# The sample tokens' depthwise convolution as one product over all shifts, one sum and one bias per chunk

## The chip, the cores and the metric

The kernel runs on one core of one Trainium2 chip. The metric is the device time of one execution in microseconds (us): the median of three runs of the kernel before is 1164.72 us (1164.26 to 1165.55). Input layout on the host is not timed.

## What is computed

One inference step of one decoder layer, for 512 prompt tokens (one sequence) and 64 sample tokens (8 sequences of 8 steps), all in float32, model width 1024:

```
x   = x + 0.5 * gate1 * SwiGLU_1(mod(rmsnorm(x)))
hm  = rmsnorm(x) * (1 + scale) + shift
proj = hm @ w_in                       # a, g (512 channels each) and u_pool (512)
u_conv   = a * sigmoid(g)
conv_ext = concat(conv_prev, u_conv)   # 30 earlier positions: zeros for the prompt, a state for the samples
v   = depthwise_causal_conv(conv_ext, w_dw) + b_dw      # 31 taps, every channel by itself
v   = silu(layernorm(v))               # over the 512 channels
p   = multi-scale pooling of u_pool
x   = x + gate * (concat(v, p) @ w_out)
x   = x + 0.5 * gate2 * SwiGLU_2(mod(rmsnorm(x)))
y   = rmsnorm(x)
```

Outputs are y for prompt and samples, and the last 30 (15) inputs of the convolution (pooling) as new states. The change concerns the line of the depthwise convolution, and of it the part of the 64 sample tokens.

## The kernel before, in words

Channels lie on the 128 partitions, tokens along the free dimension. A chunk is 128 channels; the 512 channels of the convolution are chunks 0 to 3. The 576 tokens lie in two halves of 288, each with 256 prompt columns and 32 sample columns; `prompt(t)` and `sample(t)` are views of these. The program is written by hand for each engine, in the order in which the engine runs it, with semaphores between the engines. The matrix products are float32 made of three passes (high by high, low by high, high by low), with weights split on ACT (`split_hi`, L599) and GpSimd (`split_lo`, L1118) and brought by SP's DMA queue in units of 128x2048.

The stage that matters here is the mixer, between the first and the second feed-forward part. TensorE computes six units of w_in; units 0, 2, 4 and 5 of these (`GLU`) hold a and g of chunks 0 to 3, units 1 and 3 the pooling's input. VectorE (DVE) runs this list, in this order (L1058 to L1079):

- `glu(c)` (L1024, L1026) multiplies sigmoid and TensorE's result into `conv_p` (prompt, 30 + 512 columns for each chunk) and `conv_s` (samples, 30 + 8 steps of 8 sequences = 304 columns for each chunk, step by step, the 8 sequences side by side). It frees the PSUM tile for TensorE's next unit (`tile_read[1]`).
- `conv_start(c)` (L1041, L1042) is tap 0 with the bias, one instruction for the 512 prompt columns and one for the 64 sample columns.
- `conv_taps(c, g0, g1)` (L1052, L1055) is the taps 1 to 30, in groups of 5, as a loop of DVE (`dve.Fori`) with the window's address and the wait's value computed in registers. Each tap is a scalar_tensor_tensor, v = window * w + v, for the prompt (L1052) and one for the samples (L1055). Each signals `conv_tap`, and each waits for the one before it of its own kind, since it adds to what that one wrote. A loop of a single group is written out without registers.
- The list is: glu 0, chunk 0 with glu 1 before its last group, chunk 1 with glu 2 before its last two groups, glu 3, chunk 2, an evacuation of modulation values, and of chunk 3 tap 0 and one group. The other 25 taps of chunk 3 are made by TensorE (`conv_batch`, L511, L513) as products with diagonal matrices that ACT makes (`diagonals`, L772), again one product for the prompt's 512 columns and one for the 64 sample columns. L1078 and L1079 add them.
- TensorE's `ln_sum(c)` (L525) sums a chunk over its channels as soon as it is complete. After the last one come DVE's centring (L1085), ACT's squares (L822), TensorE's sums over the tokens (L398), and the scaling, and then the product with w_out (`out_chunk`), whose chunks 0 to 3 are from the pooling and 4 to 7 from v.

GpSimd meanwhile splits weights (L1118) and makes the pooling's window sums and means (L1189 to L1229). Nothing in the program orders GpSimd's instructions against DVE's taps.

## Time and profile before

| | |
|---|---|
| median of 3 runs | 1164.72 us (1164.26 to 1165.55) |
| profiled execution: its span, first to last instruction | 1163.8 us |
| its own time beside the span | not given apart; the runs lie 0.5 to 1.8 us above the span, the median 0.9 us |
| TensorE busy | 1102.1 us, 95% |
| VectorE busy | 380.0 us, 33% |
| ScalarE busy | 317.3 us, 27% |
| GpSimd busy | 422.3 us, 36% |
| mixer's convolution on DVE | from 504.8 to 651.2 us |

The profile is of one execution. A group of instructions is read as line, engine, operation, output <- inputs, shapes, count, then busy time, mean duration in ns of one, and the engine's idle time in front of it with what ended it. A timeline row is start, duration, engine, line. DVEq is DVE's own instruction sequencer (register operations). L12 is line 12 of the kernel.

### The profile page before, as it was taken

The page shows a single profiled execution, that of the slowest core. Times are in us where ns is not written, and L with a number is a line of the kernel's source. Part 1 is how long each engine was busy: PE and PEld are TensorE (multiplying, and loading weights), DVE is VectorE, ACT ScalarE, POOL GpSimd, SP SyncE. Part 2 cuts the span into 40 slices and gives each one's busy share as a digit, 9 for nine tenths or more (in the row PEclk, how much of TensorE's full clock was granted, in tenths as well). Part 3 has the DMA queues.
Part 4 walks back from the last instruction along what each step waited for, and adds up shares of the span by engine and source line. Part 5 has one row for each costly group of instructions (what it writes and reads, how often), then busy time and mean ns, then how long its engine had stood idle before and what let it go on. Part 6 is the DMA issues. An engine that isn't in the chain of part 4 may idle for free.

```text
span 1163.8 us, 19733 instructions
## 1 busy us (share of the span) xinstructions
PE 1102.1 (95%) x8278; PEld 1057.4 (91%) x8278; DVE 380.0 (33%) x665; ACT 317.3 (27%) x358; POOL 422.3 (36%) x164
## 2 busy tenths in 40 slices
PE   8899999999999999994949799999999999999996
PEld 7799999999999999794945597999999999999996
DVE  3611111111111115689999634411111111211144
ACT  4522211222211223442224324432211222112232
POOL 2233333243332434356463032343333333433432
PEclk8999999999999999897979998999999999999998
DMA  8744222243222352242126412222222222222222
GB/s 325 288 161 181 75 107 72 98 157 112 104 73 73 109 192 98 109 182 73 37 70 177 145 51 95 74 73 78 102 73 73 92 88 72 80 101 73 72 73 81
DMA packets 21651, 127.00 MB, mean 109 GB/s; under 512 B 4192, under 2 KB 5344, under 8 KB 7008
## 3 DMA queue, kind: packets, MB, share of 16 engines
q1 hardware_dynamic: 15456, 96.06, 23.4%
q10 hardware_dynamic: 6144, 30.19, 7.3%
q8 instruction: 40, 0.66, 0.2%
q14 instruction: 11, 0.09, 0.0%
HBM read 123.06 MB, written 3.19 MB: 108 GB/s over the span
## 4 chain that ended last, share of the span: by engine, by line
PE 45%; issue 38%; POOL 7%; DVE 7%; DVEq 1%; ACT 1%; POOLq 0%; ACTq 0%
PE tile_a L352 20%; PE tile_b L352 20%; POOL w_lo L1118 6%; DVE v L1055 2%; PE ada_ps L333 2%; DVE v L1052 1%; PE tile_a L441 1%; DVE sq L937 1%; DVE sq L940 1%; PE stat_ps L398 1%; PE stat_ps L406 0%; DVEq L1055 0%; DVE hm_lo L924 0%; ACT hm_hi L631 0%; POOL w_lo L1127 0%
## 5 line engine op out<-in xcount | busy, mean ns | idle before, releaser
L1118 POOL TENSOR_TENSOR w_lo<-w_raw,w_hi 128x2048 fp32r<-128x2048 f32 x75 | 346.6, 4622 | 622.5 <-ACT w_hi L599 622.5
L352 PE MATMUL tile_b<-hm_hi,w_hi 128*128 128x288 f32 x864 | 188.2, 300 | 23.4 <-DVE conv_s L1026 23.4
L352 PE MATMUL tile_a<-hm_hi,w_hi 128*128 128x288 f32 x864 | 189.0, 301 | 13.7 <-DVE hm_lo L924 9.5
L599 ACT ACTIVATE w_hi<-w_raw 128x2048 fp32r<-128x2048 f32 x78 | 148.7, 1906 | 175.6 <-PE tile_b L352 175.5
L352 PE MATMUL tile_b<-hm_lo,w_hi 128*128 128x288 f32 x864 | 188.2, 300 | 0.0
L352 PE MATMUL tile_b<-hm_hi,w_lo 128*128 128x288 f32 x864 | 187.8, 299 | 0.0
L352 PE MATMUL tile_a<-hm_lo,w_hi 128*128 128x288 f32 x864 | 185.7, 297 | 0.0
L352 PE MATMUL tile_a<-hm_hi,w_lo 128*128 128x288 f32 x864 | 185.7, 297 | 0.0
L958 DVE TENSOR_TENSOR full<-sil,tile_b 128x576 f32<-128x576 f32 x44 | 33.2, 754 | 458.1 <-PE tile_b L352 458.1
L352 PEld LDWEIGHTS tile_b<-hm_hi,w_hi 128*128 128x128 f32 x864 | 141.8, 192 | 23.9 <-DVE conv_s L1026 23.9
L352 PEld LDWEIGHTS tile_a<-hm_hi,w_hi 128*128 128x128 f32 x864 | 139.4, 190 | 24.2 <-issue 12.1
L352 PEld LDWEIGHTS tile_b<-hm_lo,w_hi 128*128 128x128 f32 x864 | 142.4, 193 | 0.0
L352 PEld LDWEIGHTS tile_b<-hm_hi,w_lo 128*128 128x128 f32 x864 | 142.1, 192 | 0.0
L352 PEld LDWEIGHTS tile_a<-hm_lo,w_hi 128*128 128x128 f32 x864 | 140.0, 190 | 0.0
L352 PEld LDWEIGHTS tile_a<-hm_hi,w_lo 128*128 128x128 f32 x864 | 139.9, 190 | 0.0
L637 ACT ACTIVATE h_hi<-full 128x576 f32 (+1 forms) x44 | 30.1, 685 | 279.9 <-DVE full L958 279.9
L1052 DVE SCALAR_TENSOR_TENSOR v<-conv_p,vec,v 128x512 f32<-128x512 f32 x95 | 84.5, 889 | 1.8 <-DVE v L1055 0.7
L352 PE MATMUL tile_a<-h_hi,w_hi 128*128 128x288 f32 x352 | 75.6, 296 | 0.0
L352 PE MATMUL tile_b<-h_hi,w_lo 128*128 128x288 f32 x352 | 75.4, 296 | 0.0
L352 PE MATMUL tile_b<-h_hi,w_hi 128*128 128x288 f32 x352 | 75.4, 296 | 0.0
L352 PE MATMUL tile_a<-h_lo,w_hi 128*128 128x288 f32 x352 | 75.4, 296 | 0.0
L352 PE MATMUL tile_a<-h_hi,w_lo 128*128 128x288 f32 x352 | 75.4, 296 | 0.0
(146 smaller groups left out, 1138.0 us busy)
## 6 DMA issues: line engine op xcount, KB each, us to landing
w_raw<-w_units SPq DMA_DIRECT2D x78, 1024.0 KB, 4.9
ada_raw<-w_ada ACTq DMA_DIRECT2D x28, 1024.0 KB, 6.6
ada_raw<-w_ada SPq DMA_DIRECT2D x8, 1024.0 KB, 5.5
x<-x_in SPq DMA_DIRECT2D x4, 576.0 KB, 6.1
y_out<-x SPq DMA_DIRECT2D x8, 288.0 KB, 2.4
conv_s<-conv_state SPq DMA_DIRECT2D x1, 480.0 KB, 7.6
conv_s_out<-conv_s ACTq DMA_DIRECT2D x1, 480.0 KB, 7.4
wp_raw<-w_pool SPq DMA_DIRECT2D x1, 256.0 KB, 8.4
```

Source lines behind the costliest of these rows:

```text
L333: mm = pe.matmul(ada_ps[32 * g:32 * g + 32, s % 2, 0:ADA_N], cond[:, k, :], ada_raw[:, a % ADA_SLOTS, kk, ADA_N * g:ADA_N * (g + 1)], star ...
L352: mm = pe.matmul(ps[:, h, 0:HALF], w[:, w_slot, cols], r[:, k, HALF * h:HALF * (h + 1)], start=(first and n == 0), stop=(last and n == 2))
L398: mm = pe.matmul(out[:, j:j + 1], part[:, begin:begin + P], ones[:, 0:1], start=(first and j == 0), stop=(last and j == TOKEN_BLOCKS - 1))
L441: pe.transpose(tiles[t][:, 0, 0:P], ident[:], ident[:])
L599: nc.scalar.activation(w_hi[:, side, :], w_raw[:, side, :], ACT.Copy).then_inc(w_hi_ready, 1)
L637: nc.scalar.activation(h_hi[:, local, :], full[:, side, :], ACT.Copy).then_inc(h_hi_ready, 1)
L937: nc.vector.scalar_tensor_tensor(prompt(t), prompt(by_half(x[:, c, :])), gain[:, n, c, 0:1], prompt(r), ALU.mult, ALU.mult).then_inc(norm_ ...
L940: nc.vector.tensor_tensor(steps(sample(t)), steps(sample(t)), over_steps(gain[:, n, c, 1:ROWS]), ALU.mult).then_inc(norm_s2, 1)
L958: nc.vector.tensor_tensor(by_half(full[:, side, :]), by_half(sil[:]), halves(tile_b), ALU.mult).then_inc(tile_read[1], 1)
L1052: nc.vector.scalar_tensor_tensor(prompt(vc), win_p, w, prompt(vc), ALU.mult, ALU.add).then_inc(conv_tap, 1)
L1055: nc.vector.scalar_tensor_tensor(sample(vc), win_s, w, sample(vc), ALU.mult, ALU.add).then_inc(conv_tap, 1)
L1118: nc.gpsimd.tensor_tensor(w_lo[:, side, :], w_raw[:, side, :], w_hi[:, side, :].bitcast(F32), ALU.subtract).then_inc(w_lo_ready, 1)
```

## The change

For each chunk, the 31 taps of the samples become three DVE instructions: a tensor_tensor multiply over 64 columns x 31 shifts, with the input read through overlapping windows (the inner dimension steps by 8 columns) and the taps' weights repeated for all 64 columns, into a new tile `products` (128 x 64 x 31); a tensor_reduce that sums the innermost 31 into the sample columns of v; and a tensor_scalar that adds the bias, put behind the prompt's tap 0. The prompt's taps stay, and now each waits for the instruction directly in front of it. TensorE's taps of chunk 3 and the last addition keep the prompt's part alone; all 31 taps of chunk 3's samples are made on DVE. `ln_sum` waits for the new semaphore `sample_conv` besides. The size of a scratch area for dynamic DMA is set to 1024.

```diff
--- before.py
+++ after.py
@@ -148,6 +148,7 @@
         wp_raw = sb("wp_raw", [P, GROUPS * P])
         pooled_hi = sb("pooled_hi", [P, 2, TOKENS], F32R)
         pooled_lo = sb("pooled_lo", [P, 2, TOKENS], F32R)
+        products = sb("products", [P, DEC_SEQ * DEC_BATCH, WIDTH])
         mean_in = [acc, mean_b]
         four = [full[:, 0, :], full[:, 1, :], sq[:, 0, :], sq[:, 1, :]]
         eps, scrap = small[:, POOL_PAD:POOL_PAD + 1], small[:, POOL_PAD + 1:POOL_PAD + 2]
@@ -196,6 +197,7 @@
         hm_lo_ready = (sem("hm_lo_even_ready"), sem("hm_lo_odd_ready"))
 
         pads_ready, conv_tap = sem("pads_ready"), sem("conv_tap")
+        sample_products, sample_sums, sample_conv = sem("sample_products"), sem("sample_sums"), sem("sample_conv")
         pool_step, window_ready, scaled_ready, pooled_ready = (
             sem("pool_step"), sem("window_ready"), sem("scaled_ready"), sem("pooled_ready"))
         wp_hi_ready, wp_lo_ready = sem("wp_hi_ready"), sem("wp_lo_ready")
@@ -508,19 +510,17 @@
                 for kk in range(TAPS_PER_LOOP):
                     k = PE_TAP0 + b * TAPS_PER_LOOP + kk
                     pe.wait_ge(diag_ready, b * TAPS_PER_LOOP + kk + 1)
-                    pe.matmul(tile_a[:, 0, 0:SEQ], diag[:, kk, :], conv_p[:, c, k:k + SEQ],
-                              start=(k == PE_TAP0), stop=(k == WIDTH - 1))
-                    mm = pe.matmul(tile_a[:, 1, 0:DEC_BATCH * DEC_SEQ], diag[:, kk, :],
-                                   conv_s[:, c, DEC_BATCH * k:DEC_BATCH * (k + DEC_SEQ)],
+                    mm = pe.matmul(tile_a[:, 0, 0:SEQ], diag[:, kk, :], conv_p[:, c, k:k + SEQ],
                                    start=(k == PE_TAP0), stop=(k == WIDTH - 1))
                     mm.then_inc(diag_used, 1)
 
             def ln_sum(c):
 
                 if c < CONV_CHUNKS - 1:
-                    pe.wait_ge(conv_tap, 2 * WIDTH * (c + 1))
+                    pe.wait_ge(conv_tap, WIDTH * (c + 1))
                 else:
-                    pe.wait_ge(pe_taps_added, 2)
+                    pe.wait_ge(pe_taps_added, 1)
+                pe.wait_ge(sample_conv, c + 1)
                 for h in range(2):
                     mm = pe.matmul(stat_ps[:, h, 0:HALF], ones[:], v[:, c, HALF * h:HALF * (h + 1)],
                                    start=(c == 0), stop=(c == CONV_CHUNKS - 1))
@@ -1028,56 +1028,70 @@
 
             def window(c, k):
                 if isinstance(k, int):
-                    return (split2(conv_p[:, c, k:k + SEQ]),
-                            split2(conv_s[:, c, DEC_BATCH * k:DEC_BATCH * (k + DEC_SEQ)]), col(V_WDW + c * WIDTH + k))
-                return (split2(conv_p[:, c, bass.ds(k, SEQ)]),
-                        split2(conv_s[:, c, bass.ds(k * DEC_BATCH, DEC_BATCH * DEC_SEQ)]),
-                        vec[:, bass.ds(k + (V_WDW + c * WIDTH), 1)])
+                    return split2(conv_p[:, c, k:k + SEQ]), col(V_WDW + c * WIDTH + k)
+                return split2(conv_p[:, c, bass.ds(k, SEQ)]), vec[:, bass.ds(k + (V_WDW + c * WIDTH), 1)]
+
+            def conv_samples(c):
+
+                first = conv_s[:, c, 0:DEC_BATCH * DEC_SEQ]
+                windows = bass.AP(tensor=first.tensor, offset=first.offset,
+                                  ap=[first.ap[0], [1, DEC_BATCH * DEC_SEQ], [DEC_BATCH, WIDTH]])
+                taps = col(V_WDW + c * WIDTH, WIDTH).unsqueeze(1).broadcast_to([P, DEC_BATCH * DEC_SEQ, WIDTH])
+                dve.wait_ge(tile_read[1], GLU[c] + 1)
+                if c:
+                    dve.wait_ge(sample_sums, c)
+                nc.vector.tensor_tensor(products[:], windows, taps, ALU.mult).then_inc(sample_products, 1)
+                dve.wait_ge(sample_products, c + 1)
+                vc = sample(by_half(v[:, c, :]))
+                nc.vector.tensor_reduce(vc, products.rearrange("p (h n) k -> p h n k", h=2), mybir.AxisListType.X,
+                                        ALU.add).then_inc(sample_sums, 1)
+
+            def sample_bias(c):
+                vc = sample(by_half(v[:, c, :]))
+                dve.wait_ge(sample_sums, c + 1)
+                nc.vector.tensor_scalar(vc, vc, col(V_BDW + c), None, ALU.add).then_inc(sample_conv, 1)
 
             def conv_start(c):
                 vc = by_half(v[:, c, :])
-                win_p, win_s, w = window(c, 0)
+                win_p, w = window(c, 0)
                 dve.wait_ge(tile_read[1], GLU[c] + 1)
                 nc.vector.tensor_scalar(prompt(vc), win_p, w, col(V_BDW + c), ALU.mult, ALU.add).then_inc(conv_tap, 1)
-                nc.vector.tensor_scalar(sample(vc), win_s, w, col(V_BDW + c), ALU.mult, ALU.add).then_inc(conv_tap, 1)
+                sample_bias(c)
 
             def conv_taps(c, g0, g1):
                 vc = by_half(v[:, c, :])
                 with dve.Fori(g0, g1) as g:
                     for kk in range(TAPS_PER_LOOP):
-                        k = g * TAPS_PER_LOOP + (kk + 1)
-                        done = g * (2 * TAPS_PER_LOOP) + 2 * (kk + 1 + c * WIDTH)
-                        win_p, win_s, w = window(c, k)
-                        dve.wait_ge(conv_tap, done - 1)
+                        win_p, w = window(c, g * TAPS_PER_LOOP + (kk + 1))
+                        dve.wait_ge(conv_tap, g * TAPS_PER_LOOP + (kk + 1 + c * WIDTH))
                         nc.vector.scalar_tensor_tensor(prompt(vc), win_p, w, prompt(vc), ALU.mult,
                                                        ALU.add).then_inc(conv_tap, 1)
-                        dve.wait_ge(conv_tap, done)
-                        nc.vector.scalar_tensor_tensor(sample(vc), win_s, w, sample(vc), ALU.mult,
-                                                       ALU.add).then_inc(conv_tap, 1)
 
             glu(0)
             mod_evacuate(5)
+            conv_samples(0)
             conv_start(0)
             conv_taps(0, 0, TAP_GROUPS - 1)
             glu(1)
             conv_taps(0, TAP_GROUPS - 1, TAP_GROUPS)
+            conv_samples(1)
             conv_start(1)
             conv_taps(1, 0, TAP_GROUPS - 2)
             glu(2)
             conv_taps(1, TAP_GROUPS - 2, TAP_GROUPS)
             glu(3)
+            conv_samples(2)
             conv_start(2)
             conv_taps(2, 0, TAP_GROUPS)
             mod_evacuate(6)
+            conv_samples(3)
             conv_start(3)
             conv_taps(3, 0, TAP_GROUPS - PE_BATCHES)
 
             dve.wait_ge(diag_used, WIDTH - PE_TAP0)
-            dve.wait_ge(conv_tap, 2 * DVE_TAPS)
+            dve.wait_ge(conv_tap, DVE_TAPS)
             vc = by_half(v[:, CONV_CHUNKS - 1, :])
             nc.vector.tensor_tensor(prompt(vc), prompt(vc), split2(tile_a[:, 0, 0:SEQ]), ALU.add).then_inc(pe_taps_added, 1)
-            nc.vector.tensor_tensor(sample(vc), sample(vc), split2(tile_a[:, 1, 0:DEC_BATCH * DEC_SEQ]),
-                                    ALU.add).then_inc(pe_taps_added, 1)
 
             dve.wait_ge(ln_sum_done, 1)
             for c in range(CONV_CHUNKS):
@@ -1319,7 +1333,7 @@
     arrays = {k: np.ascontiguousarray(t) for k, t in arrays.items()}
     outs = {"y_out": (P, KD, TOKENS), "conv_p_out": (P, CONV_CHUNKS, CONV_PAD), "pool_p_out": (P, GROUPS, POOL_PAD),
             "conv_s_out": (P, CONV_CHUNKS, CONV_PAD * DEC_BATCH), "pool_s_out": (P, GROUPS, POOL_PAD * DEC_BATCH)}
-    nc = bacc.Bacc("TRN2", target_bir_lowering=False, num_devices=1)
+    nc = bacc.Bacc("TRN2", target_bir_lowering=False, num_devices=1, dynamic_dma_scratch_size=1024)
     args = [nc.dram_tensor(k, t.shape, mybir.dt.from_np(t.dtype), kind="ExternalInput").ap() for k, t in arrays.items()]
     args += [nc.dram_tensor(k, s, F32, kind="ExternalOutput").ap() for k, s in outs.items()]
     trunk(nc, *args)
```

## Rows read from the trace of the kernel before

**Rows 1.** The page: forty slices of the span, the granted clock in tenths.
```profile
PEclk8999999999999999897979998999999999999998
```

**Rows 2.** Waits between engines from 500 to 670 us: us in total, times, longest.
```profile
PE tile_b L352 <- DVE conv_s L1026: 23.4, 2, 15.5
...
PE stat_ps L525 <- DVE v L1079: 3.1, 1, 3.1
```

**Rows 3.** DVE's groups by form, 504 to 652 us.
```profile
L1052 DVE SCALAR_TENSOR_TENSOR v<-conv_p,vec,v 128x512 f32<-128x512 f32 x95 | 84.5, 889 | 1.8 <-DVE v L1055 0.7
L1055 DVE SCALAR_TENSOR_TENSOR v<-conv_s,vec,v 128x64 f32<-128x64 f32 x95 | 59.6, 627 | 0.0
```

**Rows 4.** DVE's timeline: taps in a loop, then taps written out.
```profile
515.12 0.75 DVE L1052 SCALAR_TENSOR_TENSOR v<-conv_p,vec,v 128x512 f32<-128x512 f32 x1
515.79 0.28 DVE L1055 SCALAR_TENSOR_TENSOR v<-conv_s,vec,v 128x64 f32<-128x64 f32 x1
516.05 0.75 DVE L1052 SCALAR_TENSOR_TENSOR v<-conv_p,vec,v 128x512 f32<-128x512 f32 x1
...
552.23 0.74 DVE L1052 SCALAR_TENSOR_TENSOR v<-conv_p,vec,v 128x512 f32<-128x512 f32 x1
552.89 0.28 DVE L1055 SCALAR_TENSOR_TENSOR v<-conv_s,vec,v 128x64 f32<-128x64 f32 x1
553.08 0.74 DVE L1052 SCALAR_TENSOR_TENSOR v<-conv_p,vec,v 128x512 f32<-128x512 f32 x1
```

**Rows 5.** Line L1052, the prompt's taps: duration min/median/max ns, first and last start.
```profile
L1052 DVE SCALAR_TENSOR_TENSOR v<-conv_p,vec,v x95: 737/752/4912, 510.9 to 649.3; 128x512 f32<-128x512 f32 x95
L1052 DVEq FUSED_REGOPS  x85: 93/93/99, 506.5 to 643.9; - x85
```

**Rows 6.** Lines L1009 and L958, DVE tensor_tensor elsewhere: duration min/median/max ns.
```profile
L1009 DVE TENSOR_TENSOR w_lo<-w_raw,w_hi x1: 1218/1218/1218, 51.4 to 51.4; 128x1024 fp32r<-128x1024 f32 x1
...
L958 DVE TENSOR_TENSOR full<-sil,tile_b x44: 753/753/756, 54.0 to 1111.9; 128x576 f32<-128x576 f32 x44
```

**Rows 7.** DVE's timeline: chunk 0's start, a tap hit twice, first and last hit tap.
```profile
505.88 0.55 DVE L1041 TENSOR_SCALAR v<-conv_p,vec 128x512 f32<-128x512 f32 x1
506.34 4.60 DVE L1042 TENSOR_SCALAR v<-conv_s,vec 128x64 f32<-128x64 f32 x1
...
519.95 0.75 DVE L1052 SCALAR_TENSOR_TENSOR v<-conv_p,vec,v 128x512 f32<-128x512 f32 x1
...
593.93 1.57 DVE L1052 SCALAR_TENSOR_TENSOR v<-conv_p,vec,v 128x512 f32<-128x512 f32 x1
595.42 0.58 DVE L1055 SCALAR_TENSOR_TENSOR v<-conv_s,vec,v 128x64 f32<-128x64 f32 x1
595.92 0.74 DVE L1052 SCALAR_TENSOR_TENSOR v<-conv_p,vec,v 128x512 f32<-128x512 f32 x1
...
638.02 1.91 DVE L1052 SCALAR_TENSOR_TENSOR v<-conv_p,vec,v 128x512 f32<-128x512 f32 x1
```

**Rows 8.** GpSimd's timeline beside these, and its gap in front of chunk 2.
```profile
506.21 4.67 POOL L1118 TENSOR_TENSOR w_lo<-w_raw,w_hi 128x2048 fp32r<-128x2048 f32 x1 [1.43 <-ACT w_hi L599]
...
594.90 1.01 POOL L1192 TENSOR_TENSOR sums<-pool_s 128x176 f32<-128x176 f32 x1
...
617.23 0.22 POOL L1206 TENSOR_TENSOR mean_b<-sums,small 128x15 f32<-128x15 f32 x1 [10.41 <-ACT mean_b L742]
```

**Rows 9.** TensorE's timeline: its last taps and the sums over channels.
```profile
641.49 2.16 PE L525 MATMUL stat_ps<-v,ones 128*128 128x288 f32 x8
645.01 1.24 PE L525 MATMUL stat_ps<-v,ones 128*128 128x288 f32 x4 [1.36 <-DVE v L1055]
651.23 1.24 PE L525 MATMUL stat_ps<-v,ones 128*128 128x288 f32 x4 [3.12 <-DVE v L1079]
```

**Rows 10.** Windows: us, busy of PE, PEld, DVE, ACT, POOL, then PEclk, DMA.
```profile
589.20:595.20 6.00, 5.96 (x25) 5.97 (x26) 6.00 (x9) 2.71 (x4) 3.11 (x3) 0.50 0.01 3
...
651.20:656.70 5.50, 5.47 (x45) 4.40 (x46) 4.09 (x6) 2.62 (x4) 0.00 (x0) 1.00 0.65 225
```

## The prediction, as it was made before the run

> **What bounds the kernel now.** I read the page's slices first. TensorE sets the pace almost everywhere, but in the slices around 490 to 670 us its granted clock drops [rows 1]. The waits of that stretch say who is late: TensorE waits for DVE's `glu` (23.4 us in two waits) and, at the end, for DVE's last addition [rows 2]. DVE itself hardly waits for anybody. So from 504.8 to 651.2 us the time is the length of DVE's list, and a microsecond put on or taken off that list moves the end of the kernel by a microsecond.
>
> Then I ask what the list is made of. 95 prompt taps are busy 84.5 us and 95 sample taps 59.6 us [rows 3]. The second number invites a false sum. A sample tap takes 0.28 us when left alone and its mean of 0.627 is made by a few that last over 4 us. And busy time isn't what an instruction adds to the chain: for that I read the distance between starts.
>
> **The loop taps, 85 of 95.** In a loop the next prompt tap starts 516.05 - 515.12 = 0.93 us after the one before; the sample tap starts 0.67 in and holds the last 0.26 [rows 4]. In the written-out groups the same pair needs only 553.08 - 552.23 = 0.85, the sample tap's slot there being 0.19 [rows 4]. The same instruction with two slots means that in the loop something else ends the slot. That is the prompt's own chain: the prompt tap lasts 0.75, and a register operation of 0.093 stands in front of each of the 85 loop taps [rows 5]; I take it to run after the wait, since the address is computed in front of the instruction itself. 0.75 + 0.093 = 0.843, and the 0.09 left to 0.93 is the semaphore's way and the issue. The sample tap lies in the shadow of that link. Taken away, the link stays, for each prompt tap adds to what the last one wrote. I cost the removal at 0 for a loop tap; the bounds are 0 and the whole 0.26 slot. For the 10 written-out taps the link has no register operation: 0.74 plus at most that 0.09 is 0.83, so 0.02 each, some 0.2 us together; bounds 0 and 0.19 each.
>
> **What is added, four times.** DVE's tensor_tensor over 1024 elements takes 1.218 us and over 576 elements 0.753 (one input there in PSUM) [rows 6], that is 1.04 ns an element. The multiply over 64 x 31 = 1984 elements is 1.218 + 960 x 0.00104 = 2.22 us. No reduction is in the trace; I take the same rate for its 1984 inputs. The reduction waits for the multiply (about 0.05 on top) and the tap behind it overlaps its end (0.07), so a chunk pays 2.27 + 2.15 = 4.4 us, and four chunks 17.6. The bias takes the place of L1042, of the same shape, at no cost. Bounds: a tensor_scalar runs at twice the rate (0.55 for 512 elements [rows 7]), and if the reduction did so too, four chunks were 13.4; twice the time for either instruction would add 8.9.
>
> That multiply steps by 8 columns from element to element, and no row reads so. The Trainium skill ("SBUF — State Buffer", in the section on Door 1) says that SBUF is read in lines of 16 bytes, and an fp32 stride above 4 elements pays for a new line at each access. By it the products would be slower; it gives no figure. No row here shows it; I keep it as a rival.
>
> **GpSimd's part.** Some DVE instructions stand still while GpSimd works: L1042 lasts 4.60 us where GpSimd's split of 4.67 us began just before [rows 7, 8]. All those that suffer are the ones whose operands lie in SBUF, while L958, with one of its inputs in PSUM, has 753 to 756 ns for all 44 although GpSimd runs beside it [rows 6]. Two effects follow.
>
> First, chunk 0. GpSimd's split wants to begin at 506.21. After the change DVE is in the multiply by then (from 505.9 to 508.0), so I let the split wait and then run to 512.5. The reduction, with one SBUF input, runs beside it if it is like L958. So about 2.0 us of the 4.4 are time in which DVE would have stood anyway: -2.0, bounds 0 and -2.1. For the other chunks there is no such cover: GpSimd has nothing from 606.8 to 617.2, which is where chunk 2's would stand, as its next work waits 10.4 us for a chain that itself begins with glu 3 [rows 8].
>
> Second, the hit taps. At 593.93 a prompt tap of 1.57 is followed by a sample tap of 0.58 at 595.42 and the next prompt tap at 595.92: 1.99 us for a tap [rows 7], with two GpSimd instructions in it, the second of which ends about 595.7 to 595.9 [rows 8]. Without the sample tap the next prompt tap can begin when GpSimd lets go, 595.7, so 0.2 earlier. In DVE's timeline from 505 to 651 us I count 27 intervals above 1.1 us with GpSimd in them, the first from 519.95, the last from 638.02 [rows 7]: 27 x 0.2 = -5.4. Bounds: 0, and 0.26 for each of the 45 GpSimd instructions that I count there, -11.7.
>
> **TensorE.** Its 25 sample products of chunk 3 go. They end at 641.5, and TensorE waits for DVE from then on [rows 9], so this is worth nothing; the cover grows further. What it costs is the clock. Before, two short waits of 1.4 and 3.1 us lead up to the last sum at 651.23, and the clock is full there (1.00 in 651.20 to 656.70) [rows 9, 10]. After, chunks 2 and 3 bring 8.8 us more on DVE behind glu 3 while TensorE has 4 us less to do: it idles about 8 us before the sum of chunk 2, and again 7 before that of chunk 3. After such a wait TensorE ran at 0.50 for 6.0 us of solid work from 589.20 to 595.20 [rows 10]. From 651.20 to 656.70 TensorE is busy 5.47 of 5.50 us, and the layer norm's next sums stand behind that in its queue. At half the clock for 5 to 6 us I lose 2.5. Bounds 0 and 3.
>
> **Sum.** +17.6 (products and sums) - 2.0 (chunk 0 under GpSimd) - 5.4 (hit taps) - 0.2 (written-out taps) - 0.1 (the last addition's sample half, less than one 0.19 slot) + 2.5 (clock) = +12.4 us. The smaller queues: SP's and GpSimd's orders aren't touched; `glu` 1 to 3 come later with DVE's list, and TensorE, ACT and GpSimd all wait there already. Each glu's PSUM tile is ready long before, as the 23.4 us of TensorE's waits show, so no new wait for TensorE rises in DVE's list. The scratch size I cost at nothing: no queue of GpSimd carries data here. Behind 651 us everything follows TensorE, so all of it reaches the end. Against the profiled execution: 1163.8 + 12.4 = 1176.2 as a span. The median stands 0.9 above this span; 1164.72 + 12.4 = 1177.1.
>
> **Rivals.**
>
> *Strided reads cost double* (15%). If each of 1984 reads takes two steps, four multiplies gain 4 x 2.07 = 8.3 us: 1177.1 + 8.3 = 1185.4. For it: no row covers such a stride. Against it: nothing but that most forms keep one element a step.
>
> *The sample taps cost their slots* (12%), the other sign. If the loop's prompt tap is not held by its wait, and the next follows when the last is done, a tap shrinks from 0.93 towards 0.67. Then 95 + 4 slots of about 0.26 vanish, -25.7, and with 17.6 - 2.0 - 0.1 on the other side and no clock loss this gives -10.2: 1154.5. The place is the link between two prompt taps, and it decides once a loop tap comes in below 0.93 - 12.4/85 = 0.78 us. The Trainium skill ("VectorE: DVE Perf Modes", section "The DRAIN you can't avoid") speaks for this side: the next Vector instruction doesn't start until the pipeline is empty, a semaphore costs nothing on top, and it is the number of instructions that should be cut. By it a loop tap would come in at its own 0.75 and the kernel gain. The trace differs: a sample tap starts 0.67 us after a prompt tap that lasts 0.75, so it doesn't wait for an empty pipe, and the two slots, 0.26 and 0.19, show a link that isn't the pipe's.
>
> *GpSimd gives back more* (10%). With one DVE instruction a tap, every GpSimd instruction finds the pause of the link: -11.7 in place of -5.4, and if the clock holds, 17.6 - 2.0 - 11.7 - 0.3 = +3.6: 1168.3.
>
> **How the numbers follow.** The forecast holds 60%: its own range, with half of the hit taps' bounds and the clock's either way, is 1172 to 1182. The rest, 3%, are odd cases near no change. The range reaches down to the third rival and up over the strided reads, 1168 to 1186, leaving the other-sign rival and the tails out. A measurement of this kernel can tell about 0.2% (2.3 us) from no change. Faster by more than that: 0.13 (the second rival and a little of its neighbourhood). Within: 0.04. Slower: 0.83.
>
> **What would show each step.** In the profile after: prompt taps in loops still 0.93 apart, with their register operation of 0.093 in front; the multiply near 2.2 us (near 4.3 if strides cost); the reduction near 2.2, and not stretched in chunk 0; chunk 0's first tap near 514.4; the hit taps about 0.2 shorter each; 651.2 moved to about 661; a granted clock of 0.5 in the stretch behind the last sum over channels. The forecast is wrong if loop taps come at 0.8 or less, or if the reduction is far from the multiply's price.

## The result and the profile after

The changed kernel takes 1175.82 us (median of 4 runs, 1173.99 to 1177.27) against 1164.79 (4 runs, 1164.26 to 1165.55): 11.0 us more, ratio 1.0092 with a 95% interval of 1.0078 to 1.0106. The forecast was 1177.1.

| us | before | after |
|---|---|---|
| span of the profiled execution | 1163.8 | 1172.2 |
| first `glu` begins | 504.81 | 502.42 |
| DVE's stretch: first `glu` to the end of the last addition | 146.4 | 156.0 |
| from there to w_out's first result read by DVE | 22.3 | 22.7 |
| the rest | 490.3 | 491.1 |

The profiled execution of the changed kernel is the fastest of its four. It reached the mixer 2.4 us earlier than the one of before, in work that the change doesn't touch: TensorE's granted clock was 1.00 in its first 60 us, and 0.91 in those of the kernel before. So its span shows 9.6 + 0.4 + 0.8 - 2.4 = 8.4 us and the medians 11.0. The stretch itself is the comparison that carries: +9.6 us. The 0.8 us in the rest are not explained.

DVE's groups by form in the changed kernel, 504 to 668 us (busy us, mean ns of one, idle before), in place of [rows 3]:

```profile
L1067 DVE SCALAR_TENSOR_TENSOR v<-conv_p,vec,v 128x512 f32<-128x512 f32 x95 | 104.4, 1099 | 14.7 <-DVE v L1067 14.3
L1043 DVE TENSOR_TENSOR products<-conv_s,vec 128x1984 f32<-128x1984 f32 x4 | 16.4, 4095 | 0.1
L1046 DVE TENSOR_REDUCE v<-products 128x64 f32<-128x1984 f32 x4 | 8.9, 2220 | 0.1
L1058 DVE TENSOR_SCALAR v<-conv_p,vec 128x512 f32<-128x512 f32 x4 | 6.4, 1588 | 0.0
```

95 sample taps of 59.6 us are gone, and the prompt's taps went from 84.5 to 104.4 us busy and from 1.8 to 14.7 us of idle in front. The idle time is what "in the shadow" looks like in a table: the pause that the sample taps had filled. The longer busy time is another thing, GpSimd's holding, which had fallen in part on the sample taps; the median prompt tap has 752 ns in both kernels. The multiply has a mean of 4.1 us, not 2.2.

DVE's timeline, quiet loop taps (start, duration, then the idle time in front), the counterpart of [rows 4]:

```profile
622.03 0.75 DVE L1067 SCALAR_TENSOR_TENSOR v<-conv_p,vec,v 128x512 f32<-128x512 f32 x1 [0.18 <-DVE v L1067]
622.96 0.75 DVE L1067 SCALAR_TENSOR_TENSOR v<-conv_p,vec,v 128x512 f32<-128x512 f32 x1 [0.18 <-DVE v L1067]
623.89 0.75 DVE L1067 SCALAR_TENSOR_TENSOR v<-conv_p,vec,v 128x512 f32<-128x512 f32 x1 [0.18 <-DVE v L1067]
```

The starts are 0.93 us apart, as they were with a sample tap between them. The link that was inferred (what lies between the end of one prompt tap and the start of the next, which adds to its result) now has a name in the profile: 0.18 us of idle, ended by the tap before. In the written-out groups the distance fell from 0.85 to 0.79; this row holds five of them, (3.89 - 0.75) / 4 = 0.785:

```profile
551.07 3.89 DVE L1067 SCALAR_TENSOR_TENSOR v<-conv_p,vec,v 128x512 f32<-128x512 f32 x5
```

The same timeline where GpSimd works, and then chunk 2's start and chunk 3's:

```profile
597.09 1.29 DVE L1067 SCALAR_TENSOR_TENSOR v<-conv_p,vec,v 128x512 f32<-128x512 f32 x1 [0.18 <-DVE v L1067]
598.56 0.79 DVE L1067 SCALAR_TENSOR_TENSOR v<-conv_p,vec,v 128x512 f32<-128x512 f32 x1 [0.18 <-DVE v L1067]
599.53 1.29 DVE L1067 SCALAR_TENSOR_TENSOR v<-conv_p,vec,v 128x512 f32<-128x512 f32 x1 [0.18 <-DVE v L1067]
601.00 0.76 DVE L1067 SCALAR_TENSOR_TENSOR v<-conv_p,vec,v 128x512 f32<-128x512 f32 x1 [0.18 <-DVE v L1067]
...
603.87 4.55 DVE L1043 TENSOR_TENSOR products<-conv_s,vec 128x1984 f32<-128x1984 f32 x1
608.46 2.22 DVE L1046 TENSOR_REDUCE v<-products 128x64 f32<-128x1984 f32 x1
610.59 2.75 DVE L1058 TENSOR_SCALAR v<-conv_p,vec 128x512 f32<-128x512 f32 x1
...
647.15 3.77 DVE L1043 TENSOR_TENSOR products<-conv_s,vec 128x1984 f32<-128x1984 f32 x1
650.95 2.22 DVE L1046 TENSOR_REDUCE v<-products 128x64 f32<-128x1984 f32 x1
```

and GpSimd's timeline beside it:

```profile
597.79 1.01 POOL L1206 TENSOR_TENSOR sums<-pool_s 128x176 f32<-128x176 f32 x1
598.88 1.39 POOL L1203 TENSOR_TENSOR sums<-sums 128x524 f32<-128x524 f32 x1
600.23 0.98 POOL L1206 TENSOR_TENSOR sums<-sums 128x160 f32<-128x160 f32 x1
...
608.52 4.54 POOL L1132 TENSOR_TENSOR w_lo<-w_raw,w_hi 128x2048 fp32r<-128x2048 f32 x1
```

Two things to see. A long GpSimd instruction (L1203 at 598.88) lengthens one tap, that of 599.53; the short one in front of it (L1206 at 597.79) hardly lengthens any: the tap at 598.56 lasts 0.79 and the next begins 0.97 later. The short instruction fits into the pause of the link. In the changed kernel 17 of the 41 intervals between taps with GpSimd in them last 0.98 us or less; before, all 32 last 1.00 or more. Before, those slots held a sample tap that was itself held [rows 7]. And chunk 2's sum, 608.46 to 610.68, has its own 2.22 us to the hundredth while GpSimd's split is running; the tensor_scalar behind it is the one that stands until 613.0.

TensorE's timeline and a window of it behind the last addition, the counterparts of [rows 9] and [rows 10]:

```profile
646.96 2.29 PE L525 MATMUL stat_ps<-v,ones 128*128 128x288 f32 x4 [13.70 <-DVE v L1067]
649.18 3.61 PE L335 MATMUL ada_ps<-ada_raw,cond 128*32 128x256 f32 x32
658.45 2.29 PE L525 MATMUL stat_ps<-v,ones 128*128 128x288 f32 x4 [5.65 <-DVE v L1094]
```

```profile
658.40:662.50 4.10, 4.05 (x20) 1.77 (x20) 1.73 (x3) 0.88 (x2) 0.00 (x0) 0.50 0.06 22
```

TensorE rests 13.7 and 5.65 us, the granted clock is 0.50 (its level of 1.2 GHz) until 662.5, and the sum over channels takes 2.29 us in place of 1.24. Yet the part behind the addition grew by 0.4 us only, which the section on the prediction takes up.

### The profile page after: what moved, and what is told of

It is laid out like the page before. It is cut to its first block, busy times and chain, and to the rows that moved or that the text cites. A ratio compares the mean times of both kernels' runs of the same rounds, so it can differ in the third digit from the quotient of the medians.

```text
span 1172.2 us, 19363 instructions
## 1 busy us (share of the span) xinstructions
PE 1090.9 (93%) x8228; PEld 1046.2 (89%) x8228; DVE 379.3 (32%) x577; ACT 316.9 (27%) x358; POOL 432.4 (37%) x164
## 4 chain that ended last, share of the span: by engine, by line
PE 43%; issue 31%; DVE 15%; POOL 8%; ACT 1%; DVEq 1%; DMA 0%; POOLq 0%; SPq 0%; ACTq 0%
PE tile_a L354 20%; PE tile_b L354 20%; DVE v L1067 9%; POOL w_lo L1132 6%; PE ada_ps L335 2%; DVE products L1043 1%; DVE sq L937 1%; DVE sq L940 1%; DVE v L1046 1%; POOL w_lo L1141 1%; DVEq L1067 1%; PE stat_ps L400 1%; POOL hm_lo L1149 0%; DMA x<-x_in 0%; DVE hm_lo L924 0%
## 5 line engine op out<-in xcount | busy, mean ns | idle before, releaser
L958 DVE TENSOR_TENSOR full<-sil,tile_b 128x576 f32<-128x576 f32 x44 | 33.2, 755 | 457.4 <-PE tile_b L354 457.4
L1067 DVE SCALAR_TENSOR_TENSOR v<-conv_p,vec,v 128x512 f32<-128x512 f32 x95 | 104.4, 1099 | 14.7 <-DVE v L1067 14.3
L354 PE MATMUL tile_b<-h_lo,w_hi 128*128 128x288 f32 x352 | 75.4, 296 | 0.0
```

The lines of the kernel that those rows point to most:

```text
L354: mm = pe.matmul(ps[:, h, 0:HALF], w[:, w_slot, cols], r[:, k, HALF * h:HALF * (h + 1)], start=(first and n == 0), stop=(last and n == 2))
L958: nc.vector.tensor_tensor(by_half(full[:, side, :]), by_half(sil[:]), halves(tile_b), ALU.mult).then_inc(tile_read[1], 1)
L1067: nc.vector.scalar_tensor_tensor(prompt(vc), win_p, w, prompt(vc), ALU.mult, ALU.add).then_inc(conv_tap, 1)
```

## The experiments

The kernel before was measured along with each group of runs: medians of 1164.97, 1164.89 and 1165.36 us. "Stretch" is DVE's stretch as in the table. Two theories stood against each other throughout. One: a prompt tap is held by its own link, and what the sample taps cost came through GpSimd alone. The other: each sample tap cost its slot. An interval is the time from one prompt tap's start to the next one's; it is called hit when a GpSimd instruction lies in it, and quiet when none does.

### The samples' multiply and sum left out

```diff
-                nc.vector.tensor_tensor(products[:], windows, taps, ALU.mult).then_inc(sample_products, 1)
...
-                nc.vector.tensor_reduce(vc, products.rearrange("p (h n) k -> p h n k", h=2), mybir.AxisListType.X,
-                                        ALU.add).then_inc(sample_sums, 1)
...
-                nc.vector.tensor_scalar(vc, vc, col(V_BDW + c), None, ALU.add).then_inc(sample_conv, 1)
+                nc.vector.tensor_scalar(vc, split2(conv_s[:, c, 0:DEC_BATCH * DEC_SEQ]), col(V_WDW + c * WIDTH),
+                                        col(V_BDW + c), ALU.mult, ALU.add).then_inc(sample_conv, 1)
```

> The changed kernel with the samples' multiply and sum left out: sample columns of v are tap 0 and the bias alone (30 of the samples' 31 taps are not computed), the prompt's taps as after the change. It tells what taking the sample taps out of the loops is worth by itself. Theory (a loop tap is held by its own chain, the sample tap lay in its shadow, and only taps that GpSimd hits get shorter): loop taps 0.93 us apart, the convolution's stretch on DVE 146.4 - 11 to 15, so 131 to 135 us, kernel about 1150 to 1154. Rival (each sample tap cost its slot of 0.26): 0.67 to 0.78 us apart, stretch 121 or less. Second rival (the removal is worth only the 5.4 us of the prediction and the rest of the gap came from elsewhere): stretch about 141.

Measured: 1153.76 us, ratio to before 0.9907 (0.9891 to 0.9924), stretch 135.4, just above the 131 to 135 expected. So the removal alone is worth 10.9 us of the stretch, and the multiply and sum cost 155.97 - 135.43 = 20.5. Quiet loop taps stay 0.93 us apart, so the slot theory falls:

```profile
572.59 0.75 DVE L1060 SCALAR_TENSOR_TENSOR v<-conv_p,vec,v 128x512 f32<-128x512 f32 x1 [0.18 <-DVE v L1060]
573.52 0.75 DVE L1060 SCALAR_TENSOR_TENSOR v<-conv_p,vec,v 128x512 f32<-128x512 f32 x1 [0.18 <-DVE v L1060]
```

Before, 32 hit intervals summed to 75.1 us, 2.35 each; here 43 summed to 73.8, 1.72 each. Above 0.93 a tap that is 45 us against 34. This split leaves out the intervals that hold a `glu` or a chunk's start, and one of those took 5.46 us here, its tap of 4.81 us beside a GpSimd split, where the same one took 1.59 before. With it GpSimd's holding fell by 7.7 us, not by 11. Another 2.3 us are quiet intervals: the 57 of before average 0.952, the 46 here 0.908. Thirteen of the 57 lasted 1.00 to 1.31 us, while here one is over 0.95 (1.06) and in the changed kernel none; what made them long is not shown. The last 1.0 us is at chunk starts and behind the last tap.

### What makes the multiply slow: three forms

```diff
# read with a step of 1
-                                  ap=[first.ap[0], [1, DEC_BATCH * DEC_SEQ], [DEC_BATCH, WIDTH]])
+                                  ap=[first.ap[0], [1, DEC_BATCH * DEC_SEQ], [1, WIDTH]])
# loops exchanged, written with a step of 31
-                                  ap=[first.ap[0], [1, DEC_BATCH * DEC_SEQ], [DEC_BATCH, WIDTH]])
-                taps = col(V_WDW + c * WIDTH, WIDTH).unsqueeze(1).broadcast_to([P, DEC_BATCH * DEC_SEQ, WIDTH])
+                                  ap=[first.ap[0], [DEC_BATCH, WIDTH], [1, DEC_BATCH * DEC_SEQ]])
+                taps = col(V_WDW + c * WIDTH, WIDTH).unsqueeze(2).broadcast_to([P, WIDTH, DEC_BATCH * DEC_SEQ])
-                nc.vector.tensor_tensor(products[:], windows, taps, ALU.mult).then_inc(sample_products, 1)
+                nc.vector.tensor_tensor(products.rearrange("p n k -> p k n"), windows, taps, ALU.mult).then_inc(sample_products, 1)
# loops exchanged, products stored [P, 31, 64], the sum reads with a step of 64
-                nc.vector.tensor_reduce(vc, products.rearrange("p (h n) k -> p h n k", h=2), mybir.AxisListType.X,
+                nc.vector.tensor_reduce(vc, products.rearrange("p k (h n) -> p h n k", h=2), mybir.AxisListType.X,
```

> The changed kernel with one number altered: the window's inner step is 1 column in place of 8 (the product is then of other columns, so the samples' convolution is not computed; the count of elements, the output and the weights' operand stay). If the step of 8 makes the multiply cost 3.8 us and not 2.2, this one takes 2.2 us where GpSimd is idle (chunk 3). If the weights' operand that repeats, the short inner dimension of 31 or the large output is the cause, it stays at 3.8.

> The changed kernel with the multiply's loops exchanged: shift outside, 64 columns inside, so the read is of adjacent columns and the output is written with a step of 31 elements; the same products lie at the same places. If only reads pay for a step, the multiply takes 2.2 us in chunk 3; if writes pay too, it stays at 3.8 or more.

> The changed kernel with the products stored shift by shift: the multiply reads and writes adjacent elements, and the sum reads with a step of 64. If a step costs wherever it is read, the multiply falls from 3.8 to 2.2 us and the sum rises from 2.2 to 3.8, and the kernel's time stays within 2 us of 1175.8. If the sum takes a step for free, the kernel is 6 us faster, about 1170. Should the step cost more at 64 than at 8, it is slower than 1175.8.

The multiply or the sum of each by line (duration min/median/max in ns, starts). With the read's step at 1:

```profile
L1043 DVE TENSOR_TENSOR products<-conv_s,vec x4: 2220/2226/3091, 504.3 to 642.9; 128x1984 f32<-128x1984 f32 x4
```

Adjacent reads, written with a step of 31:

```profile
L1043 DVE TENSOR_TENSOR products<-conv_s,vec x4: 3768/3980/4624, 504.9 to 648.4; 128x1984 f32<-128x1984 f32 x4
```

Products stored shift by shift, the sum reading with a step of 64:

```profile
L1043 DVE TENSOR_TENSOR products<-conv_s,vec x4: 2218/2226/3093, 505.8 to 645.9; 128x1984 f32<-128x1984 f32 x4
...
L1046 DVE TENSOR_REDUCE v<-products x4: 3600/3710/3786, 508.1 to 648.1; 128x64 f32<-128x1984 f32 x4
```

The step alone is the cause: where GpSimd is away the multiply takes 2.22 us at a step of 1 and 3.77 to 3.97 at 8 (chunks 3 and 1). A step on the written side costs the same, 3.77 to 3.97. The sum pays too, 3.60 to 3.72 for 2.22. The kernels took 1168.62 and 1175.56 us (one run each) and 1172.1 us (ratio 1.0059, 1.0043 to 1.0076). The last computes all that the reference does, and is 3.7 us under the changed one though the step only moved, more than the 2 us expected at most. The long instruction is now the sum, which isn't held by GpSimd (3.71 and 3.79 with it beside, 3.60 and 3.72 without), and what stands behind it, the prompt's tap 0, has a mean of 0.86 us in place of 1.59.

### TensorE kept busy

```diff
             for c in range(CONV_CHUNKS - 1):
+                if c == CONV_CHUNKS - 2:
+                    keep_warm(1, 50)
                 ln_sum(c)
             ada_products(7, 0, 2)
+            keep_warm(1, 16)
```

> The changed kernel, with TensorE given 50 idle transposes in front of the sum of chunk 2 and 16 behind it, into a tile nobody reads, so that it does not rest while DVE finishes. Theory: TensorE's clock was 0.5 in 656.0 to 662.8 after the change; kept at 1.0 the last sum over channels and the modulation product take 1.2 and 1.0 us in place of 2.3 and 1.9, and the stretch from DVE's last addition to w_out's first result is 2 us shorter, 20.7 in place of 22.7; kernel about 1174. Rival: the clock dips a little later in its place (as in the kernel before, 660.0 to 663.4), and the stretch stays at 22.3 or more: no gain.

Measured: 1176.85 us (ratio to before 1.0105), stretch 156.4, the part behind it 23.4: no gain. The filling didn't reach its aim. The transposes lasted 5.62 and 1.97 us and TensorE still rested 8.04 and 4.81 us in front of the two sums, in place of 13.7 and 5.65, and the granted clock was 0.50 from 658.6 to 665.4 all the same (TensorE's timeline, then the window):

```profile
634.52 5.62 PE L443 MATMUL tile_b<-ident 128*128 128x128 f32 x50
648.19 2.29 PE L525 MATMUL stat_ps<-v,ones 128*128 128x288 f32 x4 [8.04 <-DVE v L1070]
...
658.60:665.40 6.80, 5.71 (x27) 3.40 (x28) 4.31 (x7) 2.54 (x4) 0.00 (x0) 0.50 0.02 10
```

So this run tests neither what a TensorE without rests would get nor what a full clock would be worth there, and both stay open.

### Taps written out

```diff
# in the kernel before, and likewise in the changed one
-                with dve.Fori(g0, g1) as g:
+                for g in range(g0, g1):
```

> The kernel before, with all 95 pairs of taps written out and no loop, so without register operations. Theory: a pair then takes 0.857 us wherever GpSimd is away, 85 x 0.075 = 6 us less on DVE; kernel about 1159. That would say that in the loop the sample tap lay in a link made of the register operation. Rival: the hits of GpSimd take the gain back (it finds a DVE instruction every time), or fetching the longer program costs: within 2 us of 1165.

> The changed kernel with the prompt's taps written out, nothing else. Theory: quiet taps fall from 0.92 to 0.79; taps that GpSimd hits gain little, since the pause in which GpSimd worked for free shrinks by the same amount: 40 to 48 quiet taps x 0.13 = 5 to 6 us, kernel 1169 to 1171. Rival: all 85 gain 0.13, 11 us: 1165.

Measured: the kernel before, written out, 1158.09 us (ratio 0.9939, 0.9923 to 0.9956), stretch 140.0. The changed one, written out, 1167.07 us (10 runs; ratio 1.0015, 1.0005 to 1.0024), stretch 147.1. In DVE's timeline of the first, the pair fell to 0.86:

```profile
606.36 0.74 DVE L1052 SCALAR_TENSOR_TENSOR v<-conv_p,vec,v 128x512 f32<-128x512 f32 x1
607.02 0.27 DVE L1055 SCALAR_TENSOR_TENSOR v<-conv_s,vec,v 128x64 f32<-128x64 f32 x1
607.22 0.74 DVE L1052 SCALAR_TENSOR_TENSOR v<-conv_p,vec,v 128x512 f32<-128x512 f32 x1
```

The register operation, with the loop around it, is thus part of the link that holds a loop tap, as the prediction read it. It is the larger part: the prompt's taps alone go from 0.93 to 0.79 apart, 0.14 for a register operation of 0.093, and only 0.04 is left between a tap's 0.75 and the next start. And written out, a sample tap is no longer free: the pair takes 0.86, 0.07 more than the prompt tap alone. The changed kernel gains 8.7 us where 5 to 6 were expected and 11 was the rival: quiet taps are 0.787 (41 of them), and the hit ones (48, 1.49 each) lose only part of the pause in which GpSimd worked for free. Without the loop, samples as taps are ahead of the product by 9.0 us, much as with it (11.0).

### The prompt's accumulator in PSUM

```diff
-                nc.vector.tensor_scalar(prompt(vc), win_p, w, col(V_BDW + c), ALU.mult, ALU.add).then_inc(conv_tap, 1)
+                if c:
+                    dve.wait_ge(conv_tap, WIDTH * c)
+                nc.vector.tensor_scalar(split2(ada_ps[:, 1, :]), win_p, w, col(V_BDW + c), ALU.mult, ALU.add).then_inc(conv_tap, 1)
...
-                        nc.vector.scalar_tensor_tensor(prompt(vc), win_p, w, prompt(vc), ALU.mult,
-                                                       ALU.add).then_inc(conv_tap, 1)
+                        into = prompt(vc) if isinstance(k, int) and k == last else acc_p
+                        nc.vector.scalar_tensor_tensor(into, win_p, w, acc_p, ALU.mult, ALU.add).then_inc(conv_tap, 1)
...
-            ada_products(7, 0, 2)
             ln_sum(CONV_CHUNKS - 1).then_inc(ln_sum_done, 1)
+            ada_products(7, 0, 2)
```

The last group of each chunk is written out, so that its last tap can go to v. The first of these two runs stands on the kernel with the exchanged product, the second on the kernel before.

> The kernel of the exchanged product (multiply of adjacent columns, sum with a step of 64; 1172.1 us), with the prompt's accumulator in a PSUM bank and only the last tap of a chunk written to v. A prompt tap then has one input in SBUF and one in PSUM. TensorE's modulation product for the next stage is moved behind the last sum to free that bank. Theory: GpSimd holds only DVE instructions with two inputs in SBUF (or the doubled rate), so no prompt tap lasts over 0.8 us, the 34 us that GpSimd puts on the taps vanish, DVE's stretch falls from 152 to about 118, kernel about 1138 to 1142. Rival: GpSimd holds DVE whatever its operands, or TensorE's units and taps set the end instead: above 1160.

> The kernel before (samples as taps of 64 columns in v), with the prompt's accumulator in a PSUM bank in the same way. Theory: prompt taps are never held; a sample tap, with two inputs in SBUF, still is, and blocks the prompt tap behind it. Half the hits vanish or more; in the quiet the pair still takes 0.93. DVE's stretch 110 to 130, kernel 1130 to 1150, and under the same kernel with the product if the sample taps in the shadow are cheaper than the 5.9 us a chunk of product and sum. Rival: all hits move to the sample taps, stretch about 146 as before.

Measured with the product: 1144.62 us, ratio 0.9822 (0.9806 to 0.9838), stretch 121.7 after 152.2. Its taps by line:

```profile
L1074 DVE SCALAR_TENSOR_TENSOR ada_ps<-conv_p,vec,ada_ps x91: 742/756/757, 512.7 to 623.0; 128x512 f32<-128x512 f32 x91
L1074 DVEq FUSED_REGOPS  x70: 80/93/99, 511.6 to 609.1; - x70
```

757 ns at most, where [rows 5] had 4912, with as many GpSimd instructions beside it (47). With one operand moved to PSUM no prompt tap is held any more: the intervals between taps sum to 79.8 us for 113.9, some 2 of these 34 us because 15 more taps are written out. The stretch is 30.5 us shorter and not 34, since a part of the holding fell on the bias instructions, whose operands still lie in SBUF: the four took 6.9 us in place of 2.0. That leaves the stretch 3.7 us above the 118 expected. The part behind the stretch also grew, from 23.6 us in the kernel of the exchanged product to 26.7: ScalarE's squares stand behind a weight load whose buffer the moved TensorE product has to free. So the time is 3 us above the forecast. The waits of the changed kernel have DVE as their releaser, ScalarE's timeline of this one has that product:

```profile
ACT full L822 <- DVE v L1099: 33.1, 1, 33.1
```

```profile
631.76 0.69 ACT L822 ACTIVATE full<-v 128x576 f32<-128x576 f32 x1 [24.64 <-PE ada_ps L335]
```

With samples as taps: 1152.62 us, ratio 0.9903 (0.9880 to 0.9927), stretch 132.7 after 146.4. Its sample taps, still with both inputs in SBUF, are held in their turn and the prompt's behind them:

```profile
592.78 4.16 DVE L1060 SCALAR_TENSOR_TENSOR v<-conv_s,vec,v 128x64 f32<-128x64 f32 x1
596.87 0.73 DVE L1058 SCALAR_TENSOR_TENSOR v<-conv_p,vec,ada_ps 128x512 f32<-128x512 f32 x1
```

Here the product's form is the faster one, by 8.0 us.

### Both together

Taps written out in both of the last kernels, and behind the last sum ScalarE's weight loads moved behind its squares:

```diff
-                    with dve.Fori(g0, g1 - ends) as g:
-                        five(g)
+                    for g in range(g0, g1 - ends):
+                        five(g)
...
-            for a in range(ADA_QUARTERS * 8 - 1, ADA_QUARTERS * 8 + 1):
-                ada_load(a)
-
             act.wait_ge(pmix_lo_ready, GROUPS)
...
+            for a in range(ADA_QUARTERS * 8 - 1, ADA_QUARTERS * 8 + 1):
+                ada_load(a)
             act.wait_ge(ln_var_mm, 1)
...
             out_chunk(0)
-            out_chunk(1)
             pe.wait_ge(ln_sq_ready, CONV_CHUNKS)
...
+            out_chunk(1)
             out_chunk(2)
```

> The kernel with the product and the prompt's accumulator in PSUM (1144.6 us), with all taps written out and, behind the last sum over channels, ScalarE's two weight loads moved behind its squares and one piece of w_out's product moved behind the sums over tokens. Theory: a prompt tap alone is held by its own link, 0.75 plus register operation 0.093 plus issue; written out it takes 0.79 in place of 0.93, 76 taps x 0.14 = 10.6 us less on DVE, unless TensorE's units come late; the moved loads give 3 us back. Kernel 1131 to 1136. Rival: TensorE's units now set the pace of glu 1 to 3 and eat half of it: 1137 to 1142.

> As the run with taps written out and the prompt's accumulator in PSUM, but with the samples as taps of 64 columns, as in the kernel before. A pair takes 0.86 quiet, the sample taps are still held by GpSimd. Theory: DVE's stretch 132.6 - 6, kernel about 1146, 10 us and more above the form with the product: in a list without pauses the product is the cheaper form although it lost in the loop. Rival: within 3 us of the product's form.

Measured: with the product 1134.37 us, ratio to the kernel before 0.9728 (0.9712 to 0.9744), stretch 111.0, computing all that the reference does. With samples as taps 1146.83 us, ratio 0.9839 (0.9823 to 0.9856), stretch 126.5. The first is 31 us under the kernel before and 41 us under the changed one. The product in place of sample taps wins 12.5 us here. In the kernel with loops and the accumulator in SBUF it lost 11.0 us in its first form and 7.1 in this exchanged one (1172.1 against 1164.97). The taps written out gave 10.7 us of stretch, as expected (10.6); the moved loads gave back 1.3 us (25.4 behind the stretch for 26.7) where 3 were expected.

## Why the prediction was right, point by point

**DVE's list is the time.** Right. Stretch +9.6, medians +11.0 (0.4 of the difference behind the stretch, 0.8 in the rest, not explained); and the experiments that moved the stretch moved the kernel: with the accumulator in PSUM the stretch fell by 30.5 us and the kernel by 27.5.

**Loop taps at no gain.** Right, and the step on which the sign hung: 0.93 us before and after, with an idle of 0.18 shown. The register operation in it was confirmed by writing the taps out, and was under-sized: of the 0.18 some 0.14 went with the loop, and 0.04 was left for "the semaphore's way and the issue", for which the prediction had 0.09. So its ten written-out taps, priced at 0.02 each, had 0.06. By the rule of the Trainium skill ("VectorE: DVE Perf Modes", section "The DRAIN you can't avoid"), that the semaphore costs nothing on top, a loop tap would have come in at its own 0.75. It did not, but the 0.79 of chained taps written out is within 0.04 of it: what the rule leaves out here is the loop, more than the semaphore. No run has these taps without the wait. That the next instruction starts only on an empty pipeline is qualified in that section itself, for an instruction that isn't held, which the prediction left out; the second instruction of the pairs, at 0.66 to 0.67 us, is such a one.

**Added instructions.** The term of +17.6 was mis-sized. The sums have what was forecast, 2.22 us each. The multiplies took 3.77 to 4.55, 16.4 us for four in place of the forecast 8.9. Together 25.3 us busy, and 20.5 net of the cover by GpSimd. The failing step is the rate of 1.04 ns an element for a read with a step of 8; the rival with strided reads had the mechanism right and priced it at 2.07 us a multiply, where 1.55 (chunk 3) and 1.75 (chunk 1) were measured. The Trainium skill's rule ("SBUF — State Buffer", section on Door 1) agrees with the runs in its direction: in chunk 3 a step of 8 fp32 costs 1.70 times, steps of 31 on the written side and 64 in the sum cost 1.70 and 1.62 times. The runs add that it isn't double; no run has a step between 1 and 8, so the page's bound of 4 isn't tested.

**GpSimd's cover.** -2.0 was forecast for chunk 0 alone. The cover is 25.3 - 20.5 = 4.8 us by the difference of the two kernels. Chunk 0 has 1.4 of it: its first tap came 10.96 us behind the first `glu`, against 6.04 without the product and sum, for 6.3 us of work. The claim that chunk 2 has none failed: glu 3 came earlier against GpSimd's work than before, and its split stood beside chunk 2's sum. That sums aren't held was right.

**Hit taps.** -5.4, with -0.3 more for the written-out taps and the last addition, was mis-sized; the removal was worth -10.9. GpSimd's holding is 7.7 of it. I priced one shortened interval at one sample slot. What I missed is that the pause of the link, once empty, swallows the short GpSimd instructions whole. The other 3.2 us are no hits at all: 2.3 are quiet intervals, of which the prediction had 0.2, mostly thirteen pairs of 1.00 to 1.31 us that I hadn't looked at, and 1.0 is at chunk starts and the end. So the third rival's -11.7 is near what came in size, but not for its reason. Three readings were off besides: there are 28 intervals above 1.1 us and not 27, the first at 510.86, and the mean of the sample taps is made by four over 4 us and, for as much again, by twenty of 0.3 to 1.5 us; and a tensor_scalar, 0.54 us for 512 columns and 0.25 for 64 in the profile after, takes 0.66 ns an element, which is less than twice the rate of tensor_tensor's 1.04.

**The clock.** +2.5 became +0.4 behind the stretch. The mechanism came as said: granted clock 0.50, the sum at 2.29 for 1.24 us. But the kernel before paid for a dip of its own a little later, in the middle of w_out's first pieces, and that one is gone after (before, then after):

```profile
658.90:663.50 4.60, 4.60 (x34) 3.39 (x33) 1.42 (x3) 1.75 (x3) 0.00 (x0) 0.63 0.10 41
...
662.50:669.70 7.20, 7.20 (x60) 7.17 (x57) 2.63 (x5) 3.20 (x5) 0.00 (x0) 0.97 0.41 146
```

A cost that moves isn't a cost that is added; I had read the window up to 656.70 and not the next one.

The total is close because two errors cancel: the added instructions and their cover were 20.5 - 15.6 = 4.9 us dearer than forecast, the hit taps 10.9 - 5.7 = 5.2 us cheaper, and the clock 2.1 cheaper, so 12.4 + 4.9 - 5.2 - 2.1 = 10.0 for 9.6 + 0.4 measured. The sign rests on the loop tap's link, which the runs bear out; that the size is so close is luck.

## What to carry to other kernels

A small instruction between two chained ones may cost nothing, and taking it out may win nothing: measure the distance between starts, once with and once without whatever else differs (here loop and written-out taps), before adding up durations. When two engines hold each other, look first at which operands make them do so; moving one operand to PSUM was worth more than any recount of the work. And a change should be judged again once the real bound is gone: the product, 11 us too slow here (7 in its better form), was 12 us faster there.

## What was not expected of the hardware

- A step in an access pattern of DVE costs on either side: with GpSimd away, 2.22 us for 1984 fp32 elements at a step of 1, 3.77 to 3.97 us for a read step of 8 or a write step of 31, 3.60 to 3.72 us in a sum that reads with a step of 64.
- DVE's scalar_tensor_tensor with one input in PSUM and one in SBUF ran 91 times at 742 to 757 ns while GpSimd worked, and with both in SBUF at up to 5.15 us. Tensor_reduce from SBUF was not held in the two chunks where GpSimd's split ran beside it (2219 and 2220 ns, as without it).
- A short GpSimd instruction costs a chain of DVE taps next to nothing when the chain pauses for 0.18 us between taps: with L1206 beside it a tap lasted 0.79 us and the next began 0.97 later.
- The same chain of taps runs 0.93 us apart in a loop of DVE with addresses from registers and 0.79 us apart written out.
- Sixty-six idle transposes, 7.6 us of work, filled TensorE's two rests only in part (8.04 and 4.81 us were left), and the clock still fell to 0.50 for 6.8 us about the last sum.
